# A gated scan's level products exchanged for two token tiles at a time

## The reference, cut to what matters

```python
b = jnp.cumsum(gc, axis=3)
diff = b[..., :, None, :] - b[..., None, :, :]
decay = jnp.where(causal, jnp.exp(jnp.where(causal, diff, 0.0)), 0.0)
scores = jnp.einsum('nbhtk,nbhsk,nbhtsk->nbhts', qc, kc, decay)
o_intra = jnp.einsum('nbhts,nbhsv->nbhtv', scores, vc)
...
o_f, s_f = hgrn_scan(q, k_f, v, lf_f, s0[:, 0])
o_b, s_b = hgrn_scan(rev(q), rev(k_b), rev(v), rev(lf_b), s0[:, 1])
```

## Time and profile before

| | |
|---|---|
| median of three runs | 1646.12 us |
| the profiled execution, its own time | 1649.72 us |
| span of its instructions | 1647.9 us |
| TensorE busy | 1400.3 us (85%) |
| VectorE, ScalarE, GpSimd busy | 566.8, 358.0, 210.7 us |
| mean granted TensorE clock | 0.90 |
| predicated copies, line 1262 | 80, of 728 ns |

### The profile page before, as it was taken

One profiled execution on the slowest core, in us unless ns is written; L12 is line 12 of the kernel. 1 busy time (PEld: TensorE's weight loads), 2 busy tenths in 40 slices (PEclk: granted clock), 3 DMA queues, 4 the chain that ended last, 5 costly groups with the idle time before them and its releaser, 6 DMA issues. The chain is left out here.

```text
span 1647.9 us, 18619 instructions
## 1 busy us (share of the span) xinstructions
PE 1400.3 (85%) x6686; PEld 881.6 (53%) x6687; DVE 566.8 (34%) x1232; ACT 358.0 (22%) x777; POOL 210.7 (13%) x195
## 2 busy tenths in 40 slices
PE   3999988888899959999569999788888992999990
PEld 1577645676755534444245774566677552444440
DVE  0204623554523321111251163445454334111216
ACT  3210012333412201111151000233343110111112
POOL 0001204320000000000210002242101000000003
PEclk9999985999979869999769999689997995999995
DMA  9600023327052559999441000442301223699945
GB/s 343 218 0 4 4 102 106 107 99 297 2 206 95 195 199 332 368 363 377 173 178 27 4 1 4 154 147 91 125 4 36 100 102 115 223 369 369 368 161 204
DMA packets 114441, 262.64 MB, mean 159 GB/s; under 512 B 10152, under 2 KB 18880, under 8 KB 114368
## 3 DMA queue, kind: packets, MB, share of 16 engines
q1 hardware_dynamic: 100688, 211.84, 36.2%
q0 software_dynamic: 8064, 29.36, 4.7%
q10 hardware_dynamic: 5616, 20.45, 3.1%
HBM read 230.38 MB, written 34.41 MB: 161 GB/s over the span
## 5 line engine op out<-in xcount | busy, mean ns | idle before, releaser
L1801 PE MATMUL PS<-W,T 128*128 128x512 f32 x544 | 244.4, 603 | 4.5 <-ACT T L1854 4.5
L1801 PEld LDWEIGHTS PS<-W,T 128*128 128x128 f32 x544 | 104.9, 194 | 137.0 <-issue 131.3
L1474 PE MATMUL PS<-W,T 128*128 128x512 f32 x320 | 142.1, 598 | 0.0
L663 PE MATMUL PS<-W,hT 128*128 128x384 f32 x320 | 129.8, 487 | 0.0
L1819 PE MATMUL PS<-W,T 128*128 128x512 f32 x272 | 125.9, 607 | 1.4 <-ACT T L1878 1.4
L1020 PE MATMUL PS<-T 128*128 128x64 f32 x864 | 117.6, 292 | 3.2 <-DVE T L1237 3.2
L1020 PEld LDWEIGHTS PS<-T 128*128 128x128 f32 x864 | 110.7, 207 | 15.2 <-issue 8.3
L630 PE MATMUL PS<-hT,W 128*128 128x512 f32 x192 | 100.3, 605 | 0.0
L1919 DVE TENSOR_TENSOR T<-PS,T 128x256 f32<-128x256 f32 x34 | 14.5, 426 | 242.5 <-ACT T L1865 242.5
L1474 PEld LDWEIGHTS PS<-W,T 128*128 128x128 f32 x320 | 60.2, 193 | 69.0 <-issue 69.0
L994 PE MATMUL PS<-T 64*128 64x128 f32 (+2 forms) x480 | 67.2, 393 | 31.3 <-ACT T L1141 15.2
(11 more groups left out here) (270 smaller groups left out, 1898.5 us busy)
## 6 DMA issues: line engine op xcount, KB each, us to landing
W<-in_w_gate_up SPq DMA_DIRECT2D x34, 2048.0 KB, 12.1
W<-in_mod_w SPq DMA_DIRECT2D x19, 2048.0 KB, 8.1
W<-in_w_down SPq DMA_DIRECT2D x34, 1024.0 KB, 10.5
y_rows<-T ACTq DMA_DIRECT2D x34, 512.0 KB, 8.7
W<-in_w_in SPq DMA_DIRECT2D x8, 2048.0 KB, 14.8
W<-in_w_out SPq DMA_DIRECT2D x2, 4096.0 KB, 13.7
T<-gate_lines SPq DMA_DIRECT2D x16, 512.0 KB, 7.6
y_rows<-cst SPq DMA_DIRECT2D x1, 7680.0 KB, 27.7
```

The lines of the kernel that those rows point to most:

```text
L663: pe.matmul(out[:, 0:QW].rearrange("p (j v d) -> p j v d", v=KVH, j=G), lhsT, w[:, 0:QW].rearrange("p (v j d) -> p j v d", v=KVH, j=G), st ...
L1474: last = pe.matmul(PS[:, 4 + b, :], oT[:, t % 2, k, :], wout[:, k, half(b)], start=(k == 0), stop=(k == KC - 1))
L1801: last = pe.matmul(PS[:, 2 + par, :], hgT[:, par, k, :], w[:, k, :], start=(k == 0), stop=(k == KC - 1))
```

## The change

The five level sides of a level become three: tiles 0 and 1, tiles 2 and 3, tile 4 (`LEVEL_TILES`). A side of two tiles makes its eight products into the whole of banks 6 and 7, and one predicated copy of 128x1024 elements takes both tiles over. There are 62 sides in place of 78. The quotas are smaller: three sides in each of steps 0 to 5, two in each step from 6 on, so that no side stands behind the turning from step 6 on. The last level side is now in step 14, the last side still in step 27. The waits for the last side of a level name the last group in place of the last tile, and `merge_keys` stands ahead of the second of the three groups.

```diff
+            LEVEL_TILES = [(0, 1), (2, 3), (4,)]
+            LV_LAST = len(LEVEL_TILES) - 1
...
-                side_steps += [("level", lv, t) for t in range(NT)]
+                side_steps += [("level", lv, n) for n in range(len(LEVEL_TILES))]
...
-            quota = [(2, 2, 1)] + [(1, 1, 2) if units[u][0] == 0 else (1, 1, 0) if units[u][2] == 0 else (1, 1, 1)
-                                   for u in range(1, U)]
+            quota = [(2, 1, 0)] + [(1, 1, 1) if units[u][0] == 0 else (1, 1, 0) for u in range(1, U)]
...
-                            lv, t = at
-                            if t == 0 and lv >= 1:
+                            lv, n = at
+                            if n == 0 and lv >= 1:
...
-                            for a in range(AH):
...
-                                out = PS[:, 6 + r, col(f)]
...
+                            for m, t in enumerate(LEVEL_TILES[n]):
+                                for a in range(AH):
...
+                                    out = PS[:, 6 + r, col(2 * m + f)]
...
-                        if kind == "level" and 1 <= at[0] < NLEV - 1 and at[1] == NT - 2:
+                        if kind == "level" and 1 <= at[0] < NLEV - 1 and at[1] == LV_LAST - 1:
                             merge_keys(at[0] + 1)
...
-                            lv, t = at
+                            lv, n = at
+                            tiles = LEVEL_TILES[n]
+                            m = len(tiles)
                             dve.copy_predicated(
-                                Am[:, t, :, :],
-                                levelmask[:, lv:lv + 1, :].to_broadcast([P, AH, P]),
-                                PS[:, 6:8, 0:2 * P]).then_inc(s_free, 1)
+                                Am[:, tiles[0]:tiles[0] + m, :, :].rearrange("p t (r f) n -> p t r (f n)", r=2),
+                                levelmask[:, lv:lv + 1, :].to_broadcast([P, m * AH, P]),
+                                PS[:, 6:8, 0:2 * m * P].rearrange("p r (t n) -> p t r n", t=m)).then_inc(s_free, 1)
```

More of the change, by code:

```diff
@@ L962, in _ @@
                         if lv == 1:
-                            pool.wait_ge(s_side, side_at["level", 0, NT - 1] + 1)
+                            pool.wait_ge(s_side, side_at["level", 0, LV_LAST] + 1)
                         scale_keys(pool, lv)
-                        pool.wait_ge(s_side, side_at["level", lv, NT - 1] + 1)
+                        pool.wait_ge(s_side, side_at["level", lv, LV_LAST] + 1)
                         scale_queries(pool, lv)
@@ L1029, in side @@
                         if kind == "level":
-                            lv, t = at
-                            if t == 0 and lv >= 1:
+                            lv, n = at
+                            if n == 0 and lv >= 1:
                                 pe.wait_ge(s_hm, lv)
                                 pe.wait_ge(s_km, lv)
-                            for a in range(AH):
-                                f, r = a // 2, a % 2
-                                rows_r = slice(64 * r, 64 * r + 64)
-                                out = PS[:, 6 + r, col(f)]
[L1038 to L1047, removed]
@@ new lines, in side @@
+                            for m, t in enumerate(LEVEL_TILES[n]):
+                                for a in range(AH):
+                                    f, r = a // 2, a % 2
+                                    rows_r = slice(64 * r, 64 * r + 64)
+                                    out = PS[:, 6 + r, col(2 * m + f)]
+                                    if lv == 0:
+                                        for d in range(2):
+                                            last = pe.matmul(out, KK[rows_r, d, f, col(t)], QQ[rows_r, f, col(t)],
+                                                             start=(d == 0), stop=(d == 1))
+                                        continue
+                                    h = LEVELS[lv - 1]
+                                    at_t = f * TOK + t * P
+                                    last = pe.matmul(out, KM[lv % 2][rows_r, f * TOK + t * P:f * TOK + t * P + P],
+                                                     both_ways(QD[rows_r].rearrange("p d f n -> p d (f n)"), at_t, P, h),
+                                                     start=True, stop=True)
@@ L1135, in copy_turned @@
                         if u == FIRST_G:
-                            act.wait_ge(s_side, side_at["level", 0, NT - 1] + 1)
+                            act.wait_ge(s_side, side_at["level", 0, LV_LAST] + 1)
                         if spans_banks(u):
@@ L1148, in merge_keys @@
                         if lv >= 3:
-                            act.wait_ge(s_side, side_at["level", lv - 2, NT - 1] + 1)
+                            act.wait_ge(s_side, side_at["level", lv - 2, LV_LAST] + 1)
                         act.activation(KM[lv % 2].rearrange("p (m r j) -> p m r j", r=2, j=h),
@@ L1235, in copy_turned @@
                         if u == FIRST_G:
-                            dve.wait_ge(s_side, side_at["level", 0, NT - 1] + 1)
+                            dve.wait_ge(s_side, side_at["level", 0, LV_LAST] + 1)
                         dve.tensor_copy(turned_bufs(u)[:, 0:m], PS[:, block_at(u, 0, 0)[0], 0:m]).then_inc(s_acv, 1)
@@ L1242, in outputs @@
                         if g == LATE_TILE:
-                            dve.wait_ge(s_side, side_at["level", NLEV - 2, NT - 1] + 1)
+                            dve.wait_ge(s_side, side_at["level", NLEV - 2, LV_LAST] + 1)
                         den = rsum[:, g * GU:(g + 1) * GU]
```

## The result

The changed kernel takes 1637.03 us (median of 7 runs, 1631.93 to 1641.86), the kernel before 1646.12 (7 runs). The ratio is 0.9934, 95% interval 0.9906 to 0.9961: 0.66% faster, 9 us. The forecast was 1652.1, in the range 1638 to 1664: the time lies 1 us under the range, and the change went the other way. The profiled execution took 1638.02 us, its span is 1636.2, against 1649.72 and 1647.9.

The account below looks back on a forecast made before the run. TensorE, at 85% of the span, was taken as the bound. Idle-time changes of -3.1, +6.3 and 0.0 us made +3.2 for each layer, +6 for both, so 1652.1 us, range 1638 to 1664.

Parts of the forecast that it names:

- I leave the clock as it is in the sum: Whole stage: the granted clock was counted as unchanged, denser early exchanges raising it and stalls of steps 6 and 7 lowering it.
- the merged pair's matmuls: Merged exchange: TensorE's products for two tiles put at 1.42 us at the full clock.
- An exchange: Level sides: merged copy 1.26 us, pair waits 1.37; a merge saves 0.27 to 0.29 us where TensorE has nothing between.
- Steps 0 to 5: First stretch, each layer: TensorE's waits fall from 12.4 to 9.3 us, 3.1 us less; a `mod_turn` of 1.05 us moves in.
- the long wait behind GpSimd: Steps 0 to 5: VectorE's small operation is slow while GpSimd scales keys; TensorE's wait goes from 2.40 to 1.8 us.
- Steps 6 to 17: Second stretch, each layer: 6.3 us more, from scores of even steps 4.4, other scores 1.1, inside the steps 0.8.
- the gaps of the even steps: Scores of steps 8 to 18: no side behind the turning, about 1.0 us idle each, 6.0 us for 1.6 before.
- Steps 18 to 27: Third stretch, each layer: even, 2.1 us more ahead of scores against 2.1 less at `keys` and `state`.
- Steps 28 to 31: End of the stage: as they were; two last `out` normed at the end of step 29, where VectorE has time free.
- rival 1: Each of 32 merges saves 0.28 us and gaps fill: -9 us, 1637; or first stretch's clock gives -9. Together 0.18.
- Rival 2: Steps 6 to 8: stalls bring the clock to 1.2 GHz for 8 us or so per layer, +14 us, 1660; chance 0.38.
- A granted clock over 0.8 in steps 0 to 5: First stretch: named as a sign of being wrong, one that moves the stage by more than the forecast's sum.

Follow-up runs that it names:

- early: The kernel before with only levels 0 to 3 in pairs, new places in steps 0 to 5 and old ones from step 6: 1641.9 us, ratio 0.9948.
- split_copy: The changed kernel with two predicated copies of 128x512 in place of each merged one, TensorE's order unchanged: 1645.6 us, ratio 0.9971.
- third_place: The changed kernel with the second side of each odd step from 6 on put behind the turning: 1611.9 us, ratio 0.9769.
- late: The kernel before with only levels 4 to 7 in pairs, old places in steps 0 to 5, two sides per step from 6 on: 1684.9 us, ratio 1.0208.
- late_shift: The kernel late with one side less in step 6, so every later side stands one place further on: 1647.9 us, ratio 0.9984.
- fill_before: The kernel before with idle matmuls added ahead of the sides' waits in steps 0 to 5, nothing else: 1642.9 us, ratio 0.9956.
- fill_after: The changed kernel with idle matmuls in steps 0 to 5, two ahead of each side's wait, four where sides follow directly: 1630.4 us, ratio 0.9875.

## Why the prediction was wrong

The step that failed is the one on the clock: "I leave the clock as it is in the sum". It was the largest term of the change, some 17 us of TensorE's busy time over both layers. A second step failed beside it: the merged pair's matmuls, put at 1.42 us at the full clock, take 1.16, which is 8.3 us for 32 merges. The sum had +6 us. With -17 and -8 for these two terms, and idle times 3 us longer than forecast, that makes the -16 us of the stretches.

- **An exchange.** VectorE's part was right: 1.297 us for 1.26, and a pair waits 1.38 us at the full clock for 1.37. TensorE's part was wrong, as said: a merge is worth 0.52 us for 0.29.
- **Steps 0 to 5.** Forecast -3.1 us and the `mod_turn` on top; measured -12.7 and -6.2. About 4 us are the exchanges, as estimated above. The rest is the clock. The idle time was 13.1 and 12.3 us for a forecast of 9.3, about as much as before (12.4 and 13.3). The forecast took its waits from rows at 1.2 GHz, and at 2.4 GHz TensorE is done sooner and waits longer for the same copy. So the long wait behind GpSimd was put at 1.8 us (its own terms give 1.7) and came to 2.62:

```profile
248.49 1.84 PE L1047 MATMUL PS<-W 64*128 64x128 f32 x16 [2.62 <-DVE hT L1266]
```

That pairs raise the clock there holds wherever their TensorE order stood: 0.92, 0.83 in the changed kernel, 0.82, 0.86 in `early`, 0.83, 0.83 in `split_copy`, 0.79, 0.82 in `third_place`, with 45.4 to 49.2 us; tile by tile it was 0.62, 0.69 before, 0.72, 0.62 in `late`, 0.62, 0.69 in `late_shift`, with 55.1 to 58.2 us. That a higher clock by itself shortens the stretch is shown by `fill_before`.
- **Steps 6 to 17.** The largest term was right, the gaps of the even steps at 0.99 each. That the idle time came to 17.7 and 16.6 us for 18 is in part luck, as other terms cancel in layer 0. Ahead of step 9's scores I had 1.2 in place of 0.84, and it is 0.67 in both kernels. The pairs of `mod_rows` and `mod_turn` wait 0.9 in all for 1.9. Against that, step 6 has 1.50 for 1.15, and a wait of 1.45 us that I did not list stands in step 17, where the first `keys` follows `gate_cols`:

```profile
375.88 0.44 PE L1065 MATMUL PS<-cst,T 128*128 128x128 f32 x2 [1.45 <-ACT W L1164]
```

- **Steps 18 to 27.** Called even, and 1.8 us of idle time better in each layer: `keys` ran into no wait in even steps, and 0.32 us in odd ones at most, for my 0.1 and 0.6.
- **Steps 28 to 31.** "As they were" was wrong by -1.7 and -4.6 us: the same matmuls at 0.79 and 0.99 for 0.68 and 0.69.
- **Rivals.** The gain came from rival 1's second half, the first stretch's clock, which I had given a place but little chance. Its first half (gaps that fill themselves) is refuted: they are 0.99 us. Rival 2's mechanism is there as well. The clock fell to 1.2 GHz already in step 6, behind the wait of 1.50 us and ahead of the 2.36 of step 7, and stayed there for some 10 us in each layer; over the stretch it is 0.90 and 0.86, below the 0.96 and 0.89 before. In layer 0 that is worth at least the 3.3 us by which TensorE is busy longer. The 8 us at 1.2 GHz that rival 2 asked for were reached, but the gain of steps 0 to 5 outweighs them. A granted clock over 0.8 in steps 0 to 5, which the prediction had named as a sign of being wrong, came in both layers.

```profile
284.40:286.40 2.00, 1.53 (x18) 1.17 (x18) 0.74 (x2) 2.00 (x5) 0.00 (x0) 1.00 0.77 283
286.40:288.40 2.00, 0.90 (x8) 0.90 (x10) 1.05 (x2) 0.22 (x1) 0.00 (x0) 0.56 0.03 9
```

Why pairs hold the clock stays open. TensorE's busy time just before a fall does not tell the two kernels apart. Three stretches of the changed kernel, 3 us each, in the columns above:

```profile
240.90:243.90 3.00, 1.49 (x20) 1.29 (x20) 1.65 (x2) 0.00 (x0) 0.29 (x1) 1.00 1.05 388
243.90:246.90 3.00, 1.59 (x16) 1.29 (x16) 2.93 (x4) 0.81 (x4) 3.00 (x2) 1.00 1.04 386
246.90:249.90 3.00, 1.42 (x15) 1.42 (x16) 1.53 (x2) 1.50 (x2) 0.30 (x1) 0.86 0.20 74
```

and two of the kernel before:

```profile
233.30:236.30 3.00, 1.85 (x26) 1.47 (x23) 1.02 (x2) 1.00 (x5) 0.00 (x0) 1.00 1.05 406
236.30:239.30 3.00, 2.15 (x16) 1.86 (x16) 0.76 (x2) 0.00 (x0) 0.00 (x0) 0.60 1.04 386
```

Before, the clock fell when TensorE had just been busy 1.85 us of 3; after, it held through 1.49 and 1.59 and fell only with the long stop behind GpSimd. The idle matmuls raise it, pairs raise it, and neither tells which property of the work counts; in `late` it stayed at 1.2 GHz through 30 us in which TensorE was busy nine tenths of the time.

## What to carry to other kernels

Where a stretch runs at a low granted clock, price a change of its order by the clock first and by its idle times second, and forecast at both levels: here 4 us of exchanges in each layer came with 9 us more from the clock in one layer and 2 in the other. Price a merged group of small matmuls as one group, too: sixteen took 1.16 us where eight took 0.71. Idle matmuls in the waits test this in one run, and can be kept. A merge of small exchanges frees places in the order: put the next work where TensorE stands still for a known copy, which here was worth 25 us, nearly three times the change itself.

## What the runs showed that I had not expected

- One side less in step 6 changed the time by 37 us (`late` to `late_shift`), of which the idle time in steps 18 to 27 is 4 us a layer (15.0 to 10.8); the rest of the stretch's 22.6 us is the clock, 0.78 to 1.00, and the side work that moved.
- Stretches repeat to 0.1 us between layers where the clock is the same, and single runs of one kernel still differ by 1% (`early`: 1626.7 to 1645.3). The time outside the two stages, where every kernel here has the same instructions, runs from 1163.7 us (`third_place`) to 1176.9 (`fill_before`) in the profiles. So a difference in time of a few us says little without the stretches.
- Work added to TensorE's waits cost nothing there: `fill_after` took 45.4 us for steps 0 to 5 of layer 0 with TensorE busy 40.3 us, the changed kernel 45.4 with 32.3. The clock was 0.96 for 0.92, so a small cost may be hidden in it.
